# A hybrid convolution and mixture-of-experts layer: two weight-resident stages, phase-major tokens for the long convolution, and experts that gather token rows by slot ids

## The reference, cut to what matters

```
mod = silu(c) @ w_ada + b_ada            # 6 parts: sh1, sc1, gt1, sh2, sc2, gt2
h = rmsnorm(x, g1) * (1 + sc1) + sh1
b_a, c_a, h_a, v_b, g_b, mg_a, mg_b = split(h @ w_in)    # 512 x5, 1024 x2 columns
y_a = (b_a * dwconv3(c_a * h_a)) @ w_out_a
y_b = silu(layernorm(dwconv31(v_b * sigmoid(g_b)) + bias)) @ w_out_b
x = x + gt1 * ((sigmoid(mg_a) * y_a + sigmoid(mg_b) * y_b) @ w_o)
h2 = rmsnorm(x, g2) * (1 + sc2) + sh2
x = x + gt2 * moe(h2)                    # top-1 of 4 groups, top-2 of its 4 experts, 16 SwiGLU experts, 1024-256-1024
y = rmsnorm(x, final_g)
```

## Time and profile before

| | us |
|---|---|
| median of 3 runs | 1289.67 (1288.11 to 1290.58) |
| the profiled execution | 1294.24 |
| its span, slowest core (core 6) | 1292.6 |
| spans of the eight cores | 1271.1 to 1292.6 |
| TensorE busy | 869.2 (67%) |
| VectorE busy | 523.9 (41%) |
| ScalarE busy | 444.3 (34%) |
| GpSimd busy | 223.4 (17%) |
| moved by DMA | 198.86 MB, mean 154 GB/s |

### The profile page before, as it was taken

One profiled execution on the slowest core, in us unless ns is written; L12 is line 12 of the kernel. 1 busy time (PEld: TensorE's weight loads), 2 busy tenths in 40 slices (PEclk: granted clock), 3 DMA queues, 4 the chain that ended last, 5 costly groups with the idle time before them and its releaser, 6 DMA issues.

```text
span 1292.6 us, 17944 instructions; the slowest of 8 cores (1271.1 to 1292.6 us)
## 1 busy us (share of the span) xinstructions
PE 869.2 (67%) x5272; PEld 457.9 (35%) x5278; DVE 523.9 (41%) x1534; ACT 444.3 (34%) x728; POOL 223.4 (17%) x308
## 2 busy tenths in 40 slices
PE   0367898998899898779875344343488787882322
PEld 0233444544444444345643111121244343432321
DVE  1110446163517352656525334425244333341344
ACT  1313454365336513450662423532122221220121
POOL 1223213101120111012013110220121111004410
PEclk9999999999999999999987666566699998995675
DMA  9999949849882547068233910110499999934534
GB/s 173 170 209 215 228 142 193 250 169 318 303 160 66 192 163 131 2 231 163 87 124 55 174 64 24 66 65 9 112 182 223 223 199 210 202 89 133 154 129 150
DMA packets 135348, 198.86 MB, mean 154 GB/s; under 512 B 6992, under 2 KB 96976, under 8 KB 131920
## 3 DMA queue, kind: packets, MB, share of 16 engines
q0 software_dynamic: 111616, 136.86, 51.1%
q1 hardware_dynamic: 23632, 60.79, 15.0%
HBM read 189.69 MB, written 59.31 MB: 193 GB/s over the span
## 4 chain that ended last, share of the span: by engine, by line
PE 42%; DMA 20%; issue 13%; DVE 12%; ACT 10%; another core or an unknown queue 1%; POOL 1%; DVEq 1%; SPq 0%; ACTq 0%; POOLq 0%
PE ps_all L495 12%; DMA ring<-w_in 7%; DMA wC<-w 7%; PE ps_all L634 7%; PE ps_all L718 5%; PE ps_all L942 3%; PE ps_all L1113 2%; PE ps_all L1115 2%; PE ps_all L1128 2%; DMA vbuf<-sb 2%; DVE yrow L1136 2%; PE ps_all L702 1%; ACT L686 1%; DMA yT<-x3T 1%
## 5 line engine op out<-in xcount | busy, mean ns | idle before, releaser
L495 PE MATMUL ps_all<-hT,ring 128*128 128x448 bf16 (+1 forms) x1440 | 278.4, 353 | 55.0 <-DMA ring<-w_in 23.1
L495 PEld LDWEIGHTS ps_all<-hT,ring 128*128 128x128 bf16 x1440 | 141.4, 100 | 188.9 <-issue 80.4
L634 PE MATMUL ps_all<-ub,dgb 128*128 128x448 bf16 (+1 forms) x620 | 119.6, 338 | 15.4 <-DVE dgb L584 9.8
L356 POOL DMA_DIRECT2D ring<-wcache x104 | 55.1, 530 | 264.0 <-PE ps_all L495 141.3
L584 DVE TENSOR_SCALAR dgb<-identB,vecs_sb 128x128 bf16<-128x128 bf16 x515 | 97.1, 253 | 8.4 <-PE ps_all L634 5.8
L1128 PE MATMUL ps_all<-wC,aT 128*104 128x512 bf16 x256 | 72.5, 384 | 25.5 <-DVE yrow L1136 17.3
L634 PEld LDWEIGHTS ps_all<-ub,dgb 128*128 128x128 bf16 x620 | 60.4, 97 | 68.0 <-issue 25.5
L1177 PE MATMUL ps_all<-dgw,gat 128*128 128x128 bf16 (+1 forms) x272 | 26.9, 274 | 71.7 <-DVE x3T L1180 42.4
L1133 ACT ACTIVATE yrow<-ps_all 104x512 bf16<-104x512 f32 x64 | 38.2, 597 | 99.4 <-PE ps_all L1128 99.4
L942 PE MATMUL ps_all<-h2f,wr_sb 128*20 128x512 f32 (+2 forms) x80 | 39.3, 662 | 46.7 <-DVE h2T L933 27.8
L1136 DVE CAST yrow<-ps_all 104x512 bf16<-104x512 f32 x64 | 44.3, 692 | 51.3 <-PE ps_all L1128 42.4
(11 more groups left out here) (177 smaller groups left out, 1277.7 us busy)
## 6 DMA issues: line engine op xcount, KB each, us to landing
ring<-wcache POOLq DMA_DIRECT2D x104, 512.0 KB, 5.1
wcache<-ring POOLq DMA_DIRECT2D x26, 512.0 KB, 10.2
xslots<-dga SPq DMA_DIRECT2D x4, 3328.0 KB, 16.9
xsb<-xslots SPq DMA_DIRECT2D x16, 832.0 KB
yslots<-yrow SPq DMA_DIRECT2D x16, 832.0 KB
ring<-w_ada POOLq DMA_DIRECT2D x24, 512.0 KB, 10.6
ring<-w_in POOLq DMA_DIRECT2D x18, 512.0 KB, 13.8
wA<-w POOLq DMA_DIRECT2D x16, 512.0 KB, 17.8
```

The lines of the kernel that those rows point to most:

```text
L356: S.add(POOL, lambda e, slot=slot, bid=store_as: [e.dma_start(out=ring[slot][:, :], in_=wc_d[bid])], reads=[("wc", store_as)], writes=[("r ...
L495: return [e.matmul(PS(bank, n), wv[:, kc, j * 128:(j + 1) * 128], hT[:, kc, 0:n], start=(kc == 0), stop=(kc == NDC - 1)) for kc in range(NDC)]
L634: return [e.matmul(outp(sg_, bank), dgb[:, r, :], mv_b(sg_, c, k), start=(k == 0), stop=(k == 30)) for sg_, bank in zip(P.segs, banks)]
```

## The change

The kernel's main path is rewritten in four places. The arithmetic is the same.

1. Two stages in place of one loop. Stage 1 runs over all five passes with the ten `w_in` blocks of b, c, h, v and g resident: norm1, projections, conv A, kept as `za` and `ub` for all tokens (`hT` too). Stage 2 runs over all passes with the eight gate blocks, `w_out_a`, `w_out_b` and `w_o` resident. Between them stands conv B over all tokens and LayerNorm. No `wcache`. `x` isn't resident: it is loaded in stage 1, again in stage 2, stored after the mixer as `x2s` in DRAM and loaded at the end.
2. Phase-major tokens. The host orders a pass's tokens by phase (token index modulo 4), so columns are (phase, quad). `ub` is moved by DMAs inside SBUF to `uT`: 32 channels x 4 phases on the partitions, quads along the free dimension. Conv B is then, for each of 16 channel groups, nine matmuls with a 128x128 block (4 phases x 32 channels to 4 phases x 32 channels) of 512 columns, and nine of 16 columns for the samples. VectorE builds the nine blocks as one product of 1152 elements. LayerNorm works on that layout; its output is moved back by DMAs (`remap_out`).
3. Norm2, router and routing of pass P-1 are fillers among the gates and merges of pass P; only the last pass's come by themselves. The fence is gone. Token rows go to DRAM in order (`h2rows`); only token ids (4 bytes) are scattered to `slotid`, which is zeroed before.
4. Experts read the id table once and gather their rows by POOL's indirect DMA (four per expert, 104 rows each). Five weight buffers; the second product uses four PSUM banks. The end has three x buffers, combines in 448-column passes with tiles of 112 tokens.

The overlay of buffers is now tracked by byte ranges (`declare`, `inherit`) in place of pages.

```diff
-PASSES = [Pass(0, [Seg("p", 0, 448, 0)], False), ... Pass(4, [Seg("p", 0, 256, 1792), Seg("s", 256, 64, 2048)], True)]
+PASSES = [Pass(i, 448 * i, 112, False, (112,) * 4) for i in range(4)] + [Pass(4, 1792, 64, True, (112, 112, 96))]
...
+        n1 = norm1(PASSES[0])
+        run_all(n1["sq"])
+        n1["ss"]()
+        for hb in range(4):
+            mod_load(hb)
+        for hb in range(8):
+            mod_compute(hb)
+            if hb + 4 < 8:
+                mod_load(hb + 4)
+        W1ORD = (8, 6, 9, 7, 2, 4, 3, 5, 0, 1)
+        for i in W1ORD:
+            load_w1(i)
...
+        def build_w(i):
+            s_, G = i % WR, GORD[i]
+            op(DVE, lambda e: e.tensor_tensor(wtp[s_][:], cst[:, C_I32:C_I32 + 32].unsqueeze(1).to_broadcast([128, NB * 4, 32]),
+                                              w2t[:, G, :].unsqueeze(2).to_broadcast([128, NB * 4, 32]), ALU.mult), ["cst", "w2t_sb"], ["wtp%d" % s_], "mk_wt")
...
+        for i, G in enumerate(GORD):
...
+            S.add(PE, lambda e, G=G, bank=bank, wv=wv: [e.matmul(PS(bank), wv[:, d * 128:(d + 1) * 128], uT[:, G, d:d + 512], start=(d == 0), stop=(d == NB - 1)) for d in range(NB)],
+                  reads=["wtp%d" % s_] + uk, writes=[("ps", bank)], name="convb_mm")
+            S.add(PE, lambda e, G=G, i=i, wv=wv: [e.matmul(ps_all[:, 5, i * 16:(i + 1) * 16], wv[:, d * 128:(d + 1) * 128], uT[:, G, 520 + 16 * d:536 + 16 * d], start=(d == 0), stop=(d == NB - 1)) for d in range(NB)],
...
+        def ln_apply(G):
+            op(DVE, lambda e: e.tensor_tensor(vP[:, G, :], vP[:, G, :], lnA[:], ALU.mult), [("vT", G), "lnA"], [("vT", G)], "ln_a")
+            op(DVE, lambda e: e.tensor_tensor(vP[:, G, :], vP[:, G, :], lnB[:], ALU.add), [("vT", G), "lnB"], [("vT", G)], "ln_b")
+            op(ACT, lambda e: e.activation(out=zT[:, G, :], in_=vP[:, G, :], func=AF.Silu, bias=ccol(C_LNB + G), scale=ccol(C_LNG + G)), [("vT", G), "cst"], [("zT", G)], "zb_ev")
...
+            if P.idx == 0:
+                fill = Fill(lnf)
+                for half in range(2):
+                    for m in range(NDC):
+                        gate(P, half, m, sg0[half][:, m, 0:n], ("sg0%d" % half, m))
+                        fill(2)
+                fill.flush()
+                load_x2in(P)
+                for i in range(2):
+                    load_w("woa", woa[i], w_oa_v[:, :, i * 512:(i + 1) * 512], i)
+                    load_w("wob", wob[i], w_ob_v[:, :, i * 512:(i + 1) * 512], i)
+                for i in range(4):
+                    load_w("wo", wo[i], w_o_v[:, :, i * 256:(i + 1) * 256], i)
...
+            else:
+                n2 = norm2(PASSES[P.idx - 1])
+                if P.idx == 4:
+                    for ex in range(3):
+                        load_expert(ex)
+                fl = n2["sq"] + [nop, n2["ss"], nop, nop] + n2["apply"] + [nop, n2["router"], nop, n2["ltr"]] + chunked(n2["route"], 7) + [nop, n2["rank"]] + chunked(n2["slots"], 3)
+                fill = Fill(fl)
+                for m in range(NDC):
+                    q = 2 * (m % 2)
+                    gate(P, 0, m, sig[:, q, 0:n], ("sig", q))
+                    fill()
+                    gate(P, 1, m, sig[:, q + 1, 0:n], ("sig", q + 1))
+                    fill()
+                    ymerge(P, m, sig[:, q, 0:n], ("sig", q), sig[:, q + 1, 0:n], ("sig", q + 1), fill)
+                fill.flush()
+                run_all(n2["rows"])
+                run_all(n2["ids"])
...
-            S.add(SP, lambda e: [e.dma_start(out=xsb[b][:], in_=xs_d[ex * CAP:(ex + 1) * CAP, :].rearrange("(p t) d -> p t d", t=4))],
-                  reads=allxs, writes=["xsb%d" % b], dma=("xsl", b), ndma=1, name="ld_xs")
+            S.add(POOL, lambda e: [e.indirect_dma_start(out=xsb[b][:, t, :], out_offset=None, in_=rows_d[:, :],
+                                                        in_offset=bass.IndirectOffsetOnAxis(ap=idt[0:TP, ex, t:t + 1], axis=0),
+                                                        bounds_check=bound["t"], oob_is_err=False) for t in range(4)],
+                  reads=allrows + ["idt"], writes=[("xsb%d" % b, t) for t in range(4)], dma=("xsl", b), ndma=4, name="ld_xs")
...
-                    bank = 6 + yb["n"] % 2
+                    bank = (6, 7, 2, 3)[yb["n"] % 4]
```

1581 lines of the change are left out of this document (767 added, 814 removed).

## The result

The changed kernel takes 1184.33 us (median of 4 runs, 1171.61 to 1199.53), the kernel before beside it 1290.12 us: the ratio is 0.911, with a 95% interval of 0.905 to 0.917. The direction was right, the size was not: 106 us were gained where 305 were forecast, and 1184 lies outside 925 to 1080. Some executions of every kernel take a few per cent longer, mostly with one die at a lower granted clock; ratios, intervals and the totals called undisturbed leave these out, and where such a die would change the reading of a profile (marked * in the table of stages) the other die is read.

A forecast was written before the change was run, and what follows sets the result against it. No single engine bounds the kernel: TensorE the mixers, DMA the start and experts, chains of small waits dispatch and end. Eight stage terms, 78+149+50+92+236+57+230+93, gave 985 us; own range 940 to 1050, 8 in 10 over all cases 925 to 1080.

The forecast's parts named there:

- my 6: Long convolution: exposed time of the last ub remap, taken as 6 us between nothing and 21.
- rival (b): Stage 2: routing does not hide and fillers put TensorE out of step, +115, total 1100 us; chance 0.09.
- rival (e): Turn: each function table change costs as long again in a drain, 26 us, total 1011 us; chance 0.02.
- 3.28 MB, 15.4 us at 213 GB/s: Experts: DMA time per expert for weights, rows in and rows out, within a stage of 230 us.
- Rival (d): Experts: gathers land late behind weights, period is landing time/1.7; total 1301 us with landing at 58; chance 0.03.
- All fit beside 59: Stage 2: VectorE's 39 us and ScalarE's about 30 hide beside TensorE's 59 per pass; bubbles make it 62.
- x spilled and reloaded is hidden: Stage 2: 17 MB more of x traffic costs no time, as the DMA engines have room.
- the extra hop: Tail of norm2: scatter ids, read the id table back, gather rows; +3 us in a tail of 57.
- About 8 us until wob0 lands: Turn, after zT is free: wait for the first output weights, part of the last 31 us.
- paced by eight blocks: Turn: 64 matmuls and 64 more for w_o, held to eight weight blocks at about 3 us each.
- 13.5 MB at 185 GB/s: Start and pass 0: loading x twice, 18 weight blocks and small tables, taken as 73 of 78 us.
- do not fall together: Range 940 to 1050: bounds of start, turn, experts and final were taken not to coincide.

The follow-up runs named there:

- without late weights: Changed kernel with the weight loads of experts 5 to 15 left out: 1085 us, experts 194 us.
- with four buffers: Changed kernel with rows gathered four experts ahead into four row buffers in place of two: total 1172.7 us, experts 271 us.
- the hot row: Row 0, fetched by all 2432 empty slots; distinct ids there, against the kernel with four row buffers: 1134.9 us in place of 1172.7.
- the scattering kernels: Changed kernel with rows scattered into slots during stage 2, SP loads, four buffers, spread weight prefetch: 1101.3 us; with further edits 1060.7, 1082 and 1051.7.
- asked ahead: Ada blocks requested four ahead across passes, w2t and state copy moved from the start, against scattered rows with new turn (1060.7 us): 1051.7 us.

## Why the prediction was wrong, by its own steps

**What was right.** The stages, their order and their kinds: the convolution at 43 us (144 matmuls of 512 columns 35.3 us busy, the weight product 1.35 us of VectorE against "1.2 to 1.6", TensorE never waiting for it; the last remap's DMAs landed in medians of 3.0 to 5.1 us on the eight cores, and TensorE's wait before conv B is 2.1 us, against my 6). The turn bound by ScalarE until zT is free, 57 us against a forecast of 61, with 10 changes to silu and 10 back. TensorE's period of 12 us for an expert (11.7 after 1013, and 12.1 without late weights). Routing hidden beside the gates: TensorE is busy 60 of 64 us in the first pass and 63 of 71 in the second, so not rival (b); the third and fourth, of 73 and 77, wait for row and x2 stores. The activation that follows a table load starts at once (319, 320, 321.8 below), so not rival (e) either:

```profile
318.98 1.28 ACT L693 ACT_TABLE_LOAD   x1 [1.09 <-DVE vT L692]
320.28 1.55 ACT L693 ACTIVATE zT<-vT,cst_sb 128x528 bf16<-128x528 f32 x2
321.84 1.28 ACT L914 ACT_TABLE_LOAD   x1
```

**Experts, +57.** The step that failed is "3.28 MB, 15.4 us at 213 GB/s": it prices the gathered rows as bytes at the old rate. What they cost depended on where they came from: with four buffers the stage took 271 us with the hot row and 231 without it, where the forecast has 230, and the 209 to 229 GB/s without it bear out the old rate of 213. The other 9 us, from 280 to 271, went with the longer lead. Rival (d) named the place, and its mechanism is visible, but it is a symptom: with the lead lengthened to four experts nearly all of the time stayed. The clue was in the change before the run: a table of ids set to zero.

**Stage 2 and tail, +49 and +18.** "All fit beside 59" counted each engine's work and "x spilled and reloaded is hidden" its bytes. Neither counted that norm2 works in place on the tile that is being stored, that the rows leave through two buffers, and that three experts' weights are asked for just then. Of these the weights are shown (without them the last pass took 66 us in place of 77), the other two only together, by the scattering kernels. In the last pass the chain stands for 23.66 us on the x2 store, in the tail for 13.73:

```profile
624.16 23.66 DMA x2s<-xb
658.86 8.54 PE ps_all L774 x16
...
699.63 13.73 DMA x2s<-xb
731.68 6.27 PE ps_all L774 x16
```

The scattering kernels take back 22 to 33 us of stage 2 and 6 or 7 of the tail. What is left, 16 to 27 us of stage 2 and some 12 of the tail, stays open. For the tail the forecast had the extra hop at 3 us; no run shows that term by itself.

**Turn, +19.** The part after zT is free was mis-sized: 31 us were forecast, 54 measured. "About 8 us until wob0 lands" was 17.33, as all eight blocks are issued within 7 us, beside x. And what follows, 23 in the forecast, took 33 and was not "paced by eight blocks": TensorE ran its first output matmuls at the lower clock (1.5 us for four, 0.76 later; the granted clock of the stretch is 0.72), then waited 4.51 us for VectorE, whose merges came one each 2.06 us:

```profile
396.63 0.64 DVE merged L933
398.69 0.64 DVE merged L933
400.75 0.64 DVE merged L933
403.68 13.95 PE ps_all L941 x64
```

Grouped silus and two weights loaded early, together, give 62 us in place of 93; they were not run apart.

**Start and stage 1, +29 and +8.** I counted 13.5 MB at 185 GB/s. By 107 us 17.25 MB had landed, at 161: x of pass 2, w2t and the state's copy are in it. Of these w2t and the copy are shown: moving them, 1.2 MB, gave 6 to 7 us. Why the rate was 161 is not. In stage 1 passes 1 and 2 took 50 and 47 us against 42 each, with landings of 11.36 and 9.49 us behind POOL's halo copy, where I had allowed 2 for each pass; asked ahead, stage 1 loses 14.

**Final, +12.** TensorE waits 29.9 us for gathers; 240 GB/s was assumed, 204 were reached. Not tested further.

**The sum of all.** Seven of eight terms were too small. In all of them a transfer landed later than I let it, but not for one reason: the start had bytes that I had not counted, stage 1 a queue that stood behind a copy, the turn eight blocks issued at once, stage 2 and the tail small stores beside weights, the experts a hot row. What they share is my price, the engines' mean rate for the bytes counted. The range was built on bounds that "do not fall together"; here nearly all terms fell on the same side.

## What to carry to other kernels

Look at what the empty entries of an index table point to: padding that fetches one and the same row can cost more than the rows that are wanted. A long wait for a transfer under full DMA engines says nothing about its place in the queue; take out one kind of transfer at a time and see which one frees the engines. And for every load, ask what stands before it in its queue's program and waits for the end of something: a copy of 0.22 us kept loads back for a whole pass. And count how often a moved transfer is made: one that slips into a loop changes what the run tells.
